# The attention of the first model: two families of eight heads with fillers, rewritten as one chain of sixteen heads between weight units

## The reference, cut to what matters

```python
for i in range(DEPTH):                       # DEPTH = 2
    h = rms_norm(x, ln_attn_g[i])
    dq, dk, dv, mq, mk, mv = jnp.split(h @ w_in[i], cuts, axis=-1)    # six sections of 512 columns
    dq, dk, mq, mk = rms_norm of each over heads of 64
    y_diff = diff_attention(dq, dk, dv, lam, lam_init, ...)   # 4 heads, each a difference of two softmaxes
    y_moba = moba_attention(mq, mk, mv, bias_moba)            # 8 heads, plain causal softmax here (256 tokens)
    x = x + jnp.concatenate([y_diff, y_moba], axis=-1) @ w_out[i]
    x = x + conv_ffn(rms_norm(x, ln_ffn_g[i]), w_up[i], conv_w[i], conv_b[i], w_down[i])
```

## Time and profile before

| what | us |
|---|---|
| median of 3 runs | 2192.95 (2189.69 to 2193.74) |
| the profiled execution, its own time | 2194.73 |
| its span from first to last instruction | 2192.9 |
| PE busy in the span | 2110.8 (96%) |
| first attention stage in the trace (l = 0) | from about 57 to 176.4 |
| second attention stage (l = 1) | from about 428 to 541.6 |

### The profile page before, as it was taken

The page is one execution under the profiler, slowest core; times in us unless marked ns, Lnnn a source line. Parts: engine busy times, 40 slices in busy tenths (PEclk is TensorE's granted clock), DMA queues, the critical chain, the costliest instruction groups (busy, mean ns, idle before and its releaser), DMA issues.

```text
span 2192.9 us, 31529 instructions
## 1 busy us (share of the span) xinstructions
PE 2110.8 (96%) x12146; PEld 1815.2 (83%) x12146; DVE 1362.7 (62%) x2350; ACT 962.6 (44%) x1603; POOL 202.0 (9%) x169
## 2 busy tenths in 40 slices
PE   7899999989999999999999999999999999999998
PEld 6668998867999888888888778888778899888997
DVE  6736677674777525828454555878565578475565
ACT  4534555544555525344332453233234554445443
POOL 1410000141000100000010001111110000100100
PEclk9969999988999999999999999999999999999999
DMA  8335655522555422212122103534224234251543
GB/s 250 112 135 205 230 185 183 180 96 81 183 194 179 161 96 77 77 50 85 58 98 95 68 20 131 189 133 147 95 98 147 87 123 142 92 173 61 190 154 125
DMA packets 78811, 284.23 MB, mean 130 GB/s; under 512 B 8758, under 2 KB 9666, under 8 KB 78664
## 3 DMA queue, kind: packets, MB, share of 16 engines
q1 hardware_dynamic: 70560, 256.15, 34.5%
q10 hardware_dynamic: 6072, 18.73, 2.3%
q0 software_dynamic: 2032, 7.35, 1.2%
HBM read 276.35 MB, written 5.83 MB: 129 GB/s over the span
## 4 chain that ended last, share of the span: by engine, by line
PE 68%; DVE 8%; ACT 4%; issue 2%; POOL 0%; DVEq 0%; ACTq 0%
PE pb L927 13%; PE pb L929 13%; PE pb L928 13%; PE pb L939 5%; PE pb L941 5%; PE pb L940 5%; PE pb L945 2%; PE pb L1261 2%; PE pb L1158 2%; PE pb L1242 1%; DVE SPL L1926 1%; ACT SPH L1382 1%; PE pb L1086 1%; PE pb L973 1%; PE pb L1085 1%
## 5 line engine op out<-in xcount | busy, mean ns | idle before, releaser
L1926 DVE TENSOR_TENSOR SPL<-RAW,SPH 128x1024 fp32r<-128x1024 f32 x433 | 526.7, 1234 | 400.5 <-ACT SPH L1382 390.6
L927 PE MATMUL pb<-HTH,SPH 128*128 128x256 f32 (+1 forms) x2008 | 648.9, 323 | 7.4 <-POOL HTL L2530 2.6
L929 PE MATMUL pb<-HTH,SPL 128*128 128x256 f32 (+1 forms) x2008 | 639.3, 318 | 0.0
L928 PE MATMUL pb<-HTL,SPH 128*128 128x256 f32 (+1 forms) x2008 | 638.9, 318 | 0.0
L1382 ACT ACTIVATE SPH<-RAW 128x1024 fp32r<-128x1024 f32 x462 | 475.0, 1048 | 264.0 <-PE pb L929 116.5
L927 PEld LDWEIGHTS pb<-HTH,SPH 128*128 128x128 f32 x2008 | 383.9, 191 | 39.7 <-issue 5.9
L928 PEld LDWEIGHTS pb<-HTL,SPH 128*128 128x128 f32 x2008 | 384.2, 191 | 26.2
L929 PEld LDWEIGHTS pb<-HTH,SPL 128*128 128x128 f32 x2008 | 383.9, 191 | 26.0
L939 PE MATMUL pb<-SPH,HTH 128*128 128x512 f32 x544 | 218.7, 402 | 10.5 <-ACT QKT L1452 4.2
L940 PE MATMUL pb<-SPH,HTL 128*128 128x512 f32 x544 | 214.6, 394 | 0.0
L941 PE MATMUL pb<-SPL,HTH 128*128 128x512 f32 x544 | 214.6, 394 | 0.0
(11 more groups left out here) (276 smaller groups left out, 2825.8 us busy)
## 6 DMA issues: line engine op xcount, KB each, us to landing
RAW<-in_w_up SPq DMA_DIRECT2D x88, 512.0 KB, 4.5
RAW<-in_wa SPq DMA_DIRECT2D x64, 512.0 KB, 3.3
RAW<-in_w_in SPq DMA_DIRECT2D x48, 512.0 KB, 4.8
RAW<-in_wmg SPq DMA_DIRECT2D x48, 512.0 KB, 3.3
RAW<-in_wbr SPq DMA_DIRECT2D x48, 512.0 KB, 3.2
RAW<-in_w_down SPq DMA_DIRECT2D x44, 512.0 KB, 4.5
RAW<-in_w_ada SPq DMA_DIRECT2D x24, 512.0 KB, 4.3
ARAW<-in_w_ada ACTq DMA_DIRECT2D x24, 512.0 KB, 4.2
```

The costliest lines, as they stand in the source:

```text
L927: T.matmul(o, wh[:, kt, :], xh[:, kt, n0:n1], start=kt == 0, stop=False)
L928: T.matmul(o, wh[:, kt, :], xl[:, kt, n0:n1], start=False, stop=False)
L929: m = T.matmul(o, wl[:, kt, :], xh[:, kt, n0:n1], start=False, stop=kt == 7)
L1926: W.tensor_tensor(lo, raw, hi.bitcast(F32), SUB).then_inc(*dve.tick(s["lo_dve"], ("u", u)))
```

## The change

Sixteen heads become one chain of 19 steps (16 and three to drain). Step lists written by hand say where each goes: `FIRST = 11` says where the stage begins, `BESIDE` after which units of `w_in` a head's step stands (ten steps, heads 0 to 9), `BEHIND` what stands behind each of the eight `w_out` units: a zero is a head's step, another number is the `y_turn` of that quarter. The quarter 0 is turned after unit 23 (`EARLY_Y`). The two halves of `w_out` now run side by side, unit by unit, each with both row tiles. `qk_turn` stands three units behind its section, not four, and all sections use the ring of banks 0 to 3. Scores, turns of heads and `y_turn` share banks 4 and 5; the value sums use banks 6 and 7. All low parts of the stage are made by DVE. The fillers leave the attention: ada's steps in the feed-forward stage of l = 0 grow from 6 to 18, and norm c0 moves into the feed-forward stage of l = 1. The turned output rows lie in columns 256 to 511 of HTH and HTL, no longer in 0 to 255.

```diff
+FIRST = 11
+BESIDE = (11, 12, 14, 15, 17, 18, 20, 21, 22, 23)
+EARLY_Y = 23
+BEHIND = ((0, 0, 0), (1, 0, 0), (0, 0), (2, 0, 0), (), (3,), (), ())
-RQ = ((.8, .7, 2), (.8, 1, 3))
-GA = [2, 1]
-SPLIT_ON = ((0,), (1,))
...
+        for sec in range(6):
+            for i, _ in enumerate(self.group_n(("qkv", l, sec), f"w_in{l}", sec, (0, 1), LO4, (f"a{l}",))):
+                if i == 2 and pend is not None:
+                    for half in range(2):
+                        n = self.take(LO4, ("qkf", l, pend, half))
+                        self.add("qk_turn", l, pend, half)
+                        self.give(n)
+                    pend = None
+                if i == 3:
+                    self.add("v_copy" if sec in (2, 5) else "qk_norm", l, sec)
...
-                n = self.take((6,), ("tr", l, u - LT))
+                n = self.take((4, 5), ("tr", l, u - LT))
...
-                    self.take((7,), n)
+                    self.take((6, 7), n)
...
+        rows, heads = self.qkv(l), self.attn1(l, range(16))
+        for n, _ in enumerate(rows):
+            if n == FIRST - 1:
+                if l == 0:
+                    self.add("mask")
+                    self.add("bias_copy")
+                self.add("mark", f"attn{l}")
+            if n in BESIDE:
+                next(heads)
+            if n == EARLY_Y:
+                self.y_turn(l, 0)
+        out = [self.group_n(("wo", l, g), f"w_out{l}", g, (0, 1), LO4, ("Y", l)) for g in range(2)]
+        for unit in range(4):
+            for g in range(2):
+                next(out[g])
+                if unit == 3:
+                    for t in range(2):
+                        self.add("res1", l, g, t)
+                        self.give(("wo", l, g, t))
+                for step in BEHIND[2 * unit + g]:
+                    if step:
+                        self.y_turn(l, step)
+                    else:
+                        next(heads)
+        drain(heads)
...
-            if l == 0 and 1 <= j < 7:
+            if l == 0 and 1 <= j < 19:
                 next(self.ada)
...
+            if j == 2 and l == 1:
+                self.add("stats", "c0")
+                context = self.products("c0", LO4)
+            if 5 <= j < 13 and l == 1:
+                next(context)
```

More of the change, by code:

```diff
@@ L305, in ada_ve, with qkv @@
         yield
-    def qkv(self, l, secs, ring):
+    def qkv(self, l):
         pend = None
[L311 to L323, removed]
+        for sec in range(6):
[9 more added lines that the diff above has]
+                    for t in range(2):
+                        self.give(("qkv", l, sec, t))
+                    if sec not in (2, 5):
+                        pend = sec
+                yield
     def attn1(self, l, us):
@@ L348, in attn1, with y_turn @@
             yield
[L350 to L355, removed]
+    def y_turn(self, l, k2):
+        n = self.take((4, 5), ("yT", l, k2))
+        self.add("y_turn", l, k2)
+        self.give(n)
     def first(self):
@@ L868 @@
          "c1": (2, 3)}
-NORM_BEFORE = {"f0": "a0", "a1": "f0", "c0": "a1", "f1": "c0", "x0": "f1", "x1": "x0", "c1": "x1"}
+NORM_BEFORE = {"f0": "a0", "a1": "f0", "f1": "a1", "c0": "f1", "x0": "c0", "x1": "x0", "c1": "x1"}
 def norm_tiles(sb, tag):
@@ L934, in straight @@
         wh, wl = (a.rearrange("p (k c) -> p k c", k=2) for a in (hi, lo))
-        c = slice(t * 128, (t + 1) * 128)
+        at = t * 128 + (256 if src[0] == "Y" else 0)
+        c = slice(at, at + 128)
         for j in range(2):
@@ L1487, in y_turn @@
         act.wait_ge(s["const_dve"], ("cols", l))
-        A.activation(HH[:, k2 * 2:k2 * 2 + 2, 0:256], k.P(name)[:, :].rearrange("p (f n) -> p f n", f=2), ACT.Copy,
+        A.activation(HH[:, k2 * 2:k2 * 2 + 2, 256:512], k.P(name)[:, :].rearrange("p (f n) -> p f n", f=2), ACT.Copy,
                      scale=sb["SM"][:, 8:9] if k2 < 2 else 1.0).then_inc(*act.tick(s["qkv_act"], ("y", l, k2)))
@@ L2113, in y_turn @@
         name = ("yT", l, k2)
-        oh, ol = HH[:, k2 * 2:k2 * 2 + 2, 0:256], HL[:, k2 * 2:k2 * 2 + 2, 0:256]
+        oh, ol = HH[:, k2 * 2:k2 * 2 + 2, 256:512], HL[:, k2 * 2:k2 * 2 + 2, 256:512]
         dve.wait_ge(s["qkv_act"], ("y", l, k2))
```

## The result

The changed kernel takes 2199.96 us, median of 13 runs (2194.63 to 2203.42); the kernel before, on the same chips, 2192.95 in 13 runs. The ratio is 1.0034, 95% interval 1.0025 to 1.0042: it is slower by 0.34%, about 7 us. I had forecast 2189.4. The profiled execution of after took 2201.38 us (span 2199.6), 6.65 more than that of before.

What follows compares the result with a forecast made beforehand. PE, busy 96% of the span, was taken as the bound, losing time in attention by idling and low clock. 2194.73 + 15.5 idle - 18.8 clock - 0.3 = 2191.1 for the profiled execution, median 2189.4, range 2173 to 2204.

Steps and rivals of the forecast that it cites:

- Work that only moves: ada's eight units and c0's eight products leave attention for feed-forward; same PE cost, DVE instructions covered: net 0.
- Idle time in the attention: Both attention stages: PE idles 40.7 us against 25.2 before, 15.5 us more.
- turn of head 5: After unit 21, PE arrives 3.2 us too early, as DVE's norm, a split and head 6's scores are queued ahead.
- head 8's QKT: Head 8's scores need the first QKT copy, late behind DVE's and ACT's queued work: PE waits 4.0 us.
- first `w_out` unit: It reads `y_turn` 0, which stands directly ahead, so PE waits for HTL: 2.8 us.
- the triple: Steps of heads 10, 11, 12 in a row in `w_out`; head 12's scores wait for a bank: 4.7 us.
- `y_turn` 3: It stands directly ahead of `w_out` unit 3, which waits for it: 1.5 us, as before.
- Clock: Attention stages: three low stretches of 3.4 us per layer cost 10.2 us against 29.0 before, 18.8 us back.
- Rival 1: Dense units hold the clock and DVE keeps up in attention: 2171, or 2179 by clock alone; chance 0.28.
- Rival 2: Triple step and pairs keep the clock low in `w_out`: 2205 for both layers, 2197 for one; 0.28 with Rival 3.
- Rival 3: DVE's queue, 92% full, brings attention waits to their upper bound of 55 us: 2203; chance 0.28 with Rival 2.
- Rival 4: Moved ada work hurts the feed-forward stage through added transfers, PE waiting 1 us in 12 steps: 2201; chance 0.04.

Runs made afterwards that it cites:

- statistics in parts: Changed kernel, c0's statistics on DVE in three parts (steps 2, 3, 4), products one step later: 2197.04 us, ratio 1.0021; at steps 2, 4, 5 with late `y`: 2190.67.
- late `y`: Changed kernel with the first family's y (norm of 3.5 us on DVE) one step later, behind the next head's probs: 2193.16 us, ratio 1.0003.
- early turns: Changed kernel with late `y`, statistics in parts, `y_turn` 0 ahead of head 9's step and `y_turn` 3 one unit earlier: 2179.05 us, ratio 0.9936.
- the best kernel: Changed kernel with late `y`, c0's statistics at steps 2, 4 and 5, and both early turns: 2179.05 us, ratio 0.9936.
- the spread triple: Changed kernel with head steps behind the `w_out` units laid out as 2, 2, 2, 2, 1 in place of 3, 2, 2, 2: 2199.93 us, ratio 1.0037.
- separate banks: Changed kernel with turns of heads in bank 6, value sums in bank 7, scores in banks 4 and 5: 2202.20 us, ratio 1.0049.
- POOL: Changed kernel with low parts made by POOL again from unit 14 of `w_in` to the middle of `w_out`: 2199.45 us, ratio 1.0029.

## Why the prediction was wrong

Two terms failed. The clock was to give back 18.8 us and gave 12.2, and "Work that only moves", put at net 0, cost 4.0 us by a wait and a low stretch behind DVE's piece for `c0`, and some 3 us of PE's own time for `ada`.

**The sum, term by term** (for the profiled executions: forecast -3.6, measured +6.65; their spans differ by 6.7). Over the whole span PE idles 2199.6 - 2104.2 = 95.4 us instead of 82.1. In all low stretches together it is busy for 59.5 us instead of 83.8, so the clock gives 12.2 back. What is left of its busy time, counted at the full clock, is 2074.5 instead of 2068.9, for the same 12146 products. So 13.3 - 12.2 + 5.6 = 6.7, where the forecast had 15.2 - 18.8 + 0 = -3.6: idle time 1.9 better, the clock 6.6 worse, and 5.6 us of own work that stood at nothing.

- *Idle time in the attention: right, and a little too much.* Forecast 15.5 us more, measured 12.6. Five places were named with their releasers: turn of head 5, 3.2 forecast and 3.18 measured; head 8's QKT 4.0 and 2.06 or 3.04; first `w_out` unit 2.8 and 2.51; the triple 4.7 and 3.41; `y_turn` 3 1.5 and 1.50. Walking through the two in-order queues with durations of the earlier trace rows is what found them. There is some luck in the sum: 2.93 of the 12.6 us are the wait at the start of the first stage, which was 0.3 to 3.2 us in the other traces of the chain, and the turn of head 5 waits 1.7 to 2.0 us in the first stage of six of them.
- *Clock: the largest term of the error, mis-sized.* Forecast 18.8 us back in the attention, measured 29.0 - 18.2 = 10.8. The kind of change was right (short stretches in place of the 24 us ones), the size not. I took the shortest stretch seen, 3.4 us, at three places. There were four places in each stage, since the turn of head 5, whose wait I had forecast, also lowers the clock, and four of the eight stretches lasted 6.8 us. These 8 us alone turn the forecast of -3.6 into +4.4, the wrong sign.
- *"Work that only moves ... Net 0": the step that failed in its reasoning.* For `c0`, one part alone gives 1.0038. I had written that its few instructions on DVE are covered, since DVE is busy 133 of 190 us. Three mistakes are in it. The row is the first feed-forward stage's, while `c0` moves to the second, where DVE is busy 145.14 of 197.5 us, and 8.37 of 10.0 around the place. The few instructions are 27 and take DVE 9.8 us in that stage (145.14 to 154.91). And the mean says nothing of one piece of 4.2 us in an in-order queue, where a step of the stage leaves DVE some 2 us (an estimate: 52.4 us idle over its 24 steps): the split behind it came late, and PE lost 2.3 us of idle time and 1.7 us by the low stretch behind it, 4.0 that the term had at nothing. The products' own 4 us came on top, and the attention stage without them was only 3.0 us shorter, since the low clock lasted longer there.
- For `ada` the total came out even (1.0001), the term did not: its stage grew by 8.4 us where 6 were forecast, and its work took PE about 5.5 us of full clock in the attention. That is half of the 5.6 us of own work; the other half is spread over the attention's products and not assigned.

**The rivals.** Rival 1 (the clock held) did not come. Rival 2 asked for a low clock past `w_out`'s third unit, which begins at 146.0; the last low stretch of the first stage ends at 139.2, so no. Rival 3 (more idle time) no, it was less. Rival 4 expected waits in the first feed-forward stage: `ada`'s transfers did no harm, idle time there is 1.9 us as before. DVE in the second feed-forward stage was in none of them, and none had a clock that falls more often and a little longer than in the centre. The sign was wrong at a chance of 0.27; the time is inside the range.

**What is shown and what is argued.** Shown by one part alone: moving `c0` makes the kernel before as slow as the whole change does. That it is the whole cause is not shown: with `c0` back in the attention the chain is still at 1.0025. The two losses do not add up (0.38% and 0.25% against 0.34% for both), and the chain with both fillers left in the attention was not run. Shown by the statistics in parts: the wait comes from the piece's length, and with its low stretch it is 3.7 of the 8.2 us. Shown by late `y` and early turns: the order of the heads' work on DVE holds 18 us. The larger part of that is idle time, which falls from 37.8 to 24.2 us in the two attention stages from after to the best kernel, while the cost of the low clock there falls from 18.2 to 15.2. Argued only: why the clock stayed low longer when the triple's wait was spread.

## What to carry to other kernels

A mean busy share hides what an in-order queue can take: before putting a piece of several microseconds on an engine, compare it with what one step leaves free in the very stage where it goes, and see what is queued behind it. Work that serves as filler can give back less where it leaves than it costs where it goes (`c0`: 3.0 us against 8.1), so count what it gives back by its stage's length without it, not by its own duration. Count short low stretches one by one behind every wait that you forecast, and allow for twice the shortest one seen. And the order within a queue (a late `y`, a turn one step earlier) was worth more here than who does the splits or which banks are used.

## What the runs showed of the hardware

- In the attention stages of the kernels with the chain the clock fell for 3.4, 6.8 or 10.2 us each time (before, for 23.9 us too), and shorter waits could be followed by a longer low stretch (3.41 us of waiting and 6.8 us low; 0.80 + 1.31 and 10.2 us).
- The same wait of 2.15 us in the second feed-forward stage was followed by 3.4 us of low clock in three kernels (after, the spread triple, `c0` alone moved) and by none in three others (separate banks, late `y`, POOL). With separate banks and with POOL that stage, which there has no low stretch at its start either, took 203.5 us instead of 205.7.
- An operation of 4 elements on each partition took 2.30 us on DVE while POOL was in a split, 0.17 us without.
